# Retention projections of two heads as seven block products over half of the depth

## The reference, cut to what matters

```python
h = rms_norm(x, norm1_g)
proj = h @ w_in                     # 2048 x 7168: retention q,k,v,gate and attention q,k,v, 8 heads of 128 each
rq, rk, rv, rg, aq, ak, av = split(proj)
ret = silu(rg) * head_group_norm(retention(rotary(rq), rotary(rk), rv), ret_norm_g)
att = chunk_attention(rms_norm(aq, q_norm_g), rms_norm(ak, k_norm_g), av, rel_bias)
x = x + concat([ret, att]) @ w_out
h = rms_norm(x, norm2_g)
x = x + square(relu(h @ w_ff1)) @ w_ff2      # 2048 -> 8192 -> 2048
```

## Time and profile before

| what | value |
|---|---|
| time, median of 3 runs | 1113.13 us (1112.95 to 1113.15) |
| the profiled execution's own time | 1113.28 us |
| its span, first to last instruction | 1111.2 us |
| around the span | 2.1 us |
| busy share of PE, DVE, ACT, POOL | 99%, 75%, 59%, 5% |
| granted TensorE clock, mean | 1.000 |
| moved by DMA | 253 MB, 228 GB/s over the span |

### The profile page before, as it was taken

The page is one execution under the profiler, slowest core; times in us unless marked ns, Lnnn a source line. Parts: engine busy times, 40 slices in busy tenths (PEclk is TensorE's granted clock), DMA queues, the critical chain, the costliest instruction groups (busy, mean ns, idle before and its releaser), DMA issues.

```text
span 1111.2 us, 13678 instructions
## 1 busy us (share of the span) xinstructions
PE 1105.2 (99%) x5234; PEld 942.2 (85%) x5234; DVE 830.8 (75%) x828; ACT 657.3 (59%) x765; POOL 51.5 (5%) x58
## 2 busy tenths in 40 slices
PE   9999999999999999999999999999999999999998
PEld 8889899899898888888888888888888888888887
DVE  6667566576576668869787869787869787869783
ACT  6544544554554556677655577665577665577662
POOL 0100000000000000000000000000000000000000
PEclk9999999999999999999999999999999999999999
DMA  9855455454464556787797787797787797787792
GB/s 362 319 191 180 151 198 179 151 197 153 156 217 152 204 208 182 266 278 220 246 290 222 258 277 221 243 291 221 259 279 220 244 291 221 259 277 219 246 278 86
DMA packets 39551, 253.14 MB, mean 228 GB/s; under 512 B 4432, under 2 KB 4944, under 8 KB 12624
## 3 DMA queue, kind: packets, MB, share of 16 engines
q1 hardware_dynamic: 34464, 218.12, 53.4%
q0 software_dynamic: 4608, 33.56, 16.0%
q10 hardware_dynamic: 432, 0.81, 0.2%
HBM read 250.37 MB, written 2.10 MB: 227 GB/s over the span
## 4 chain that ended last, share of the span: by engine, by line
PE 99%; DMA 0%; ACT 0%; DVE 0%; ACTq 0%; issue 0%
PE acc L489 11%; PE acc L496 11%; PE acc L503 11%; PE acc L667 10%; PE acc L665 10%; PE acc L663 10%; PE bankC L643 4%; PE acc L643 4%; PE acc L638 4%; PE bankC L638 4%; PE bankC L636 4%; PE acc L636 4%; PE bankD L643 1%; PE bankD L638 1%; PE bankD L636 1%; PE acc L687 1%
## 5 line engine op out<-in xcount | busy, mean ns | idle before, releaser
L1311 DVE TENSOR_TENSOR w_lo<-raw,w_hi 128x2048 fp32r<-128x2048 f32 x180 | 410.9, 2289 | 126.8 <-ACT w_hi L924 126.6
L924 ACT ACTIVATE w_hi<-raw 128x2048 fp32r<-128x2048 f32 x180 | 344.8, 1917 | 220.8 <-PE acc L667 145.9
L1118 DVE TENSOR_TENSOR w_lo<-raw,w_hi 128x1024 fp32r<-128x1024 f32 (+1 forms) x152 | 167.8, 1107 | 68.6 <-ACT w_hi L767 68.5
L767 ACT ACTIVATE w_hi<-raw 128x1024 fp32r<-128x1024 f32 (+1 forms) x152 | 142.9, 962 | 34.3 <-PE acc L503 25.3
L489 PE MATMUL acc<-w_hi,hT_hi 128*128 128x512 f32 (+1 forms) x512 | 129.5, 374 | 0.8 <-ACT w_hi L767 0.8
L496 PE MATMUL acc<-w_hi,hT_lo 128*128 128x512 f32 (+1 forms) x512 | 123.5, 362 | 0.0
L503 PE MATMUL acc<-w_lo,hT_hi 128*128 128x512 f32 (+1 forms) x512 | 123.2, 362 | 0.0
L496 PEld LDWEIGHTS acc<-w_hi,hT_lo 128*128 128x128 f32 x512 | 93.5, 188 | 10.5
L503 PEld LDWEIGHTS acc<-w_lo,hT_hi 128*128 128x128 f32 x512 | 93.4, 188 | 10.0
L663 PE MATMUL acc<-w_hi,hF_hi 128*128 128x512 f32 x256 | 100.8, 394 | 0.0
L663 PE MATMUL acc<-w_hi,dF_hi 128*128 128x512 f32 x256 | 99.9, 390 | 0.0
(11 more groups left out here) (187 smaller groups left out, 1573.4 us busy)
## 6 DMA issues: line engine op xcount, KB each, us to landing
raw<-in_w_up SPq DMA_DIRECT2D x64, 1024.0 KB, 6.4
raw<-in_w_down SPq DMA_DIRECT2D x64, 1024.0 KB, 6.5
raw<-in_w_ret SPq DMA_DIRECT2D x32, 1024.0 KB, 4.7
raw<-in_w_att SPq DMA_DIRECT2D x28, 768.0 KB, 4.4
raw<-in_w_out SPq DMA_DIRECT2D x16, 1024.0 KB, 4.7
raw<-in_w_up POOLq DMA_DIRECT2D x16, 1024.0 KB, 8.6
raw<-in_w_down POOLq DMA_DIRECT2D x16, 1024.0 KB, 8.9
raw<-in_w_att SPq DMA_DIRECT2D x6, 384.0 KB, 7.7
```

Of the source, the lines that this page charges most:

```text
L767: nc.scalar.activation(piece(w_hi, q, 0, PIECE_KT * n), raw[:, q // 2, (q % 2) * PIECE_KT * n:(q % 2 + 1) * PIECE_KT * n], ACT.Copy).then_ ...
L924: nc.scalar.activation(w_hi[:, ring(s)], raw[:, r, :], ACT.Copy).then_inc(slab_hi, 1)
L1118: nc.vector.tensor_tensor(piece(w_lo, q, 0, PIECE_KT * n), raw[:, q // 2, (q % 2) * PIECE_KT * n:(q % 2 + 1) * PIECE_KT * n], piece(w_hi, ...
L1311: nc.vector.tensor_tensor(w_lo[:, ring(s)], raw[:, r, :], w_hi[:, ring(s)].bitcast(f32), ALU.subtract).then_inc(slab_lo, 1)
```

## The change

Attention projections stay as they are. The retention projections of two heads (blocks of the loop `i` in 0 to 3) are now computed together. The part of them over depth tiles 0 to 7 is a 2 by 2 block of weight slabs, a and b above, e and d below (a and e belong to the first column block, b and d to the second), and takes seven products of 12 matmuls: Q1 (a), P5 (a+b), P6 (a+b+d), P7 (b+d), P3 (d), Q2 (e), P4 (a+b+d+e). Each writes a single bank. Depth tiles 8 to 15 are computed as before, with 24 matmuls a slab: Z1, Z2 for one head, H1, H2 for the other. A block runs these 19 slabs, 38 pieces, on every engine:

```diff
+        def in_free(i, step, m):
+            ...
+            elif step == "P5":
+                pe.wait_ge(sf_lo_ok, 1)
+                if i:
+                    pe.wait_ge(p5_kept, i)
+            elif step == "P6":
+                pe.wait_ge(sf_lo_ok, 2)
+                pe.wait_ge(q1_kept, i + 1)
+            elif step == "P7":
+                pe.wait_ge(sf_lo_ok, 3)
+                pe.wait_ge(z_set, i + 1)
+            elif step == "P3":
+                pe.wait_ge(sf_lo_ok, 4)
+            elif step == "Z1" and m == 1:
+                pe.wait_ge(w_set, i + 1)
+            elif step == "Q2":
+                pe.wait_ge(h_set, i + 1)
+            elif step == "P4":
+                pe.wait_ge(y_set, i + 1)
...
+                for bank, m in banks:
+                    if half == 0:
+                        in_free(i, step, m)
+                    for t in tiles:
+                        fresh = step in ("I0", "J0", "Q1", "P5") and t == 0
+                        wide = N if fresh else n
+                        start = (t - 2 * half) * n
+                        nc.tensor.matmul(bank[:, 0:wide], stationary(step, m, t)[0], piece(w_hi, q, start, start + wide),
+                                         start=fresh, stop=False, skip_group_check=True)
...
+            def in_hi(q):
+                i, step, half = in_step(q)
+                ...
+                elif half == 0 and step == "P5":
+                    act.wait_ge(in_summed, 4 * i + 1)
+                elif half == 0 and step == "P6":
+                    act.wait_ge(in_summed, 4 * i + 2)
+                elif half == 0 and step == "P7":
+                    act.wait_ge(in_summed, 4 * i + 3)
+                elif half == 0 and step == "P4":
+                    act.wait_ge(in_summed, 4 * i + 4)
...
+            def in_sum(i, into, other, read):
+                r, o = IN_PLAN[i, into][0], IN_PLAN[i, other]
+                dve.wait_ge(in_raw[o[0]], o[1])
+                dve.wait_ge(lo_done, in_first(i, read) + 2)
+                nc.vector.tensor_tensor(raw[:, r, :], raw[:, r, :], raw[:, o[0], :], ALU.add).then_inc(in_summed, 1)
...
+                at_piece(i, 10, att_mean_squares, h)
+                at_piece(i, 10, in_sum, i, "a", "b", "Q1")
...
+            load_group(G_OUT, w_out, 0, N)
+            sp.wait_ge(piece_used, in_first(BLOCKS - 1, "P3") + 2)
+            for c in range(OUT_GROUPS):
+                sp.dma_start(xs[:, :, c * N:(c + 1) * N], x_rows[:, :, c * N:(c + 1) * N]).then_inc(x_in[c], 16)
...
+            def last_slab(p, step):
+                ...
+                for m, bank, first, end in ((0, bH, 0, N), (1, bY, 0, half), (1, bX, half, N)):
+                    for t in range(SLAB_KT):
+                        cols = slice(t * N + first, t * N + end)
...
+                    dve.wait_ge(half_used, 2 * prev + 4)
+                    both = xs[:, 1, c * N:(c + 1) * N]
+                    nc.vector.tensor_tensor(both, bY[:], both, ALU.add).then_inc(acc_read_dve, 1)
+                    dve.wait_ge(acc_read_dve, added(prev) + 4)
+                    dve.wait_ge(slab_used, slab_no(prev, "H2") + 1)
+                    right = xs[:, 1, c * N + half:(c + 1) * N]
+                    nc.vector.tensor_tensor(right, bX[:, half:N], right, ALU.add).then_inc(acc_read_dve, 1)
```

More of the change, by code:

```diff
@@ L419, in _ @@
             for p in (PAIRS - 2, PAIRS - 1):
-                for n in range(4):
+                for n in range(4 if p < PAIRS - 1 else 3):
                     c, m = 2 * (p % 2) + (n < 2), n % 2
@@ L423, in _ @@
                     sp.dma_start(out_rows[:, m, c * N:(c + 1) * N], xs[:, m, c * N:(c + 1) * N]).then_inc(stored, 16)
-            sp.wait_ge(stored, 4 * MT * 16)
+            for half in range(2):
+                first = (OUT_GROUPS - 2) * N + half * (N // 2)
+                sp.wait_ge(acc_read_dve, added(PAIRS - 1) + 4 + half)
+                sp.dma_start(out_rows[:, 1, first:first + N // 2], xs[:, 1, first:first + N // 2]).then_inc(stored, 16)
+            sp.wait_ge(stored, (4 * MT + 1) * 16)
         @block.gpsimd
@@ new lines, in _ @@
+            for q in range(8 * G_OUT):
+                nxt = q + AHEAD
+                if nxt < PIECES:
+                    x_hi(nxt)
+                if nxt < 8 * G_OUT:
+                    in_hi(nxt)
+                else:
+                    hi_piece(G_OUT, nxt - 8 * G_OUT, N)
+                if q == PIECES:
+                    act.wait_ge(gq_ok, 1)
+                for f in work.get(q, ()):
+                    f()
+            group(G_OUT, N, N, {j: work.get(8 * G_OUT + j, []) for j in range(PIECES)})
```

622 lines of the change are left out of this document (440 added, 182 removed).

## The result

The changed kernel takes 1137.84 us (median of 4 runs, 1137.68 to 1138.35), the kernel before 1113.07 (1112.95 to 1113.15): a ratio of 1.0223, 95% interval 1.0206 to 1.0241. It is 24.8 us slower. The forecast was 1134.8, in a range of 1119 to 1145.

The account below looks back on a forecast made before the run. TensorE, busy 1105.2 of 1111.2 us, was taken as the bound. From 1113.3: -10.0 for matmuls, +23.2 for block waits, +8.7 for the first block, -0.4 at the end gave 1134.8 us, range 1119 to 1145.

Parts of the forecast that it names:

- C: Transposes of each block's first retention head: TensorE waits for VectorE's rotation and addition, 1.9 us a block.
- A: Transposes of each block's first attention head: TensorE waits for scaled q and k behind sum a+b, 1.3 us.
- low part 25: Around Z1: TensorE waits for VectorE's low part of piece 25, made after the fourth sum, 0.6 us a block.
- bank subtraction: Z1's second row tile: TensorE waits for VectorE's subtraction after the low part of piece 26, 0.9 us a block.
- The block without waits: Block of two heads with fewer matmuls and no new waits: 82.7 us against 85.2, kernel 10.0 us less.
- The first block: Activation sums at pieces 8 to 15 add waits of 3.5 and 4.5 us and small ones: +8.7 us.
- The tail: Program's end: narrower last matmuls +0.2 us, shorter last add and store, net -0.4 us (-0.7 to +1.2).
- The signs: In the profile: some 32 us of TensorE waits on VectorE, blocks about 88.5 us, VectorE near 85%, feed-forward unchanged.
- Waits hidden: Rival: VectorE and ScalarE running ahead of TensorE cover the blocks' waits, time 1102.9 us; chance 0.10.
- B: Around Z1: TensorE waits 0.6 us for low part 25, 0.9 for the bank subtraction, 0.7 for scaled q and k.
- Slabs late: Rival: slab e lands late in each block, lengthening the wait around Z1, +7 us, 1142; chance 0.12.
- The clock falls: Rival: in the first block TensorE's long standstills bring 1.2 GHz for pieces 12 and 13, up to +8 us; chance 0.10.

Follow-up runs that it names:

- the kernel with every order mended: Changed kernel with rotation, fourth sum, activation sums, both heads' squares and scaling, and softmaxes all moved, nothing left out: 1115.88 us, ratio 1.0025.
- the kernel with the new first block: The kernel with every order mended, plus ScalarE, GpSimd and VectorE steps of its first block reordered: 1112.60 us, ratio 0.9996.

## Why the prediction was right, step by step

**Direction and mechanism: right.** The matmuls removed were worth less than the waits that the added work made, with VectorE busy 80% on average. Runs showed it, not the trace alone: with the same matmuls and the waits mended the time falls by 26.9 us (1137.84 to 1110.90), which is more than the 24.8 lost. Of the orders turned alone, C gave 7.4 us and the activation sums 5.1, both about as expected.

**The waits of a block: right in sum, and nearly one by one.** Measured as the distance beyond the usual spacing in the second block: A 1.35 (forecast 1.3), first softmax 0.27 (0.3), low part 25 0.66 (0.6), bank subtraction 0.73 (0.9), second head's q and k 0.57 (0.7), second softmax 0.23 (0.1), C 1.96 (1.9). The sum is 5.77 against 5.8. That it agrees to 0.03 is luck, since single steps are off by up to 0.2.

**The block without waits: this term was too small.** I put it at 82.7 us, from matmul counts times spacing. The block is 89.3 with 5.8 of waits, so 83.5 without. The kernel whose one labelled wait is 0.22 us still takes 83.96, or 83.7 without it. So the removed matmuls were worth 1.5 to 1.7 us a block and not 2.5, which is some 3.2 us over four blocks and about as much as the forecast was short (1137.8 - 1134.8 = 3.0). Part of it can be seen: a product's piece of six matmuls takes 1.37 to 1.39 us and not 1.36, and behind each wait the first matmuls of a piece are up to 0.1 us further apart. The rest lies in steps of 0.1 that I did not assign, so it stays open.

**The first block: right within 1 us, in part by luck.** From the same point of the program it takes 98.7 us, against a forecast of 97.2; 0.8 of the difference is the block's base. Its two long waits come where they were walked: 3.2 us (forecast 3.5), and 3.5 for a_qk (4.5). At full clock the second would have been 5.3, since the slow piece 12 fills 1.8 us of it; the scaling came late because VectorE waited 0.91 us for GpSimd's power, which the walk has as covered. The slow clock adds 1.4 us behind it, which the sum has at nothing, and so the smaller waits must be below the 2.3 us put for them. These errors nearly cancel.

```profile
35.23 0.73 PE L740 MATMUL bankC<-w_lo,hT_hi 128*128 128x512 f32 x2 [3.17 <-DVE w_lo L1393]
35.99 1.51 PE L727 MATMUL acc<-w_hi,hT_hi 128*128 128x384 f32 x4
...
43.43 0.69 PE L612 MATMUL bankA<-ident,a_qk 128*128 128x128 f32 x2 [3.52 <-DVE a_qk L1476]
```

**The tail: right.** The matmuls of 256 columns stand 0.120 us apart in the kernel after, and its end is 0.3 us shorter than before (forecast 0.4). The edit alone in the kernel before gives 0.65 us, inside the bounds of the term, but there the store gave 0.6, more than the 0.4 allowed for it.

**The signs.** From its first product to the end of the span the feed-forward stage takes 688.9 us (689.2 before), as forecast. VectorE is busy 81% between 100 and 350 us, not near 85%. The profile's list has 24.0 us of waits and not 32, since it counts idle time alone: in the second block it has 1.16 for A and 1.79 for C, where the distances have 1.35 and 1.96.

**The rivals.** *Waits hidden*: no, and the one thing it claimed, that a lead covers them, failed at A, B and C alike. *Slabs late*: no, VectorE waited 0.3 us once for the DMA of a retention slab in the whole run. *The clock falls*: it did, with 0.66 and 0.70 granted behind the two long waits, so part of TensorE's time there is at 1.2 GHz. I gave it 0.10, and it came; its price was what I had wrong. I put up to 8 us on it. Piece 12 took 3.9 us and not 2.1, but behind it TensorE waited for a_qk in any case. Only piece 13 and the transposes counted, 1.4 us, and of these 0.7 came back when the clock was held up. The Trainium skill (TensorE: Matmul & The Clock Gate, "Why this matters for your kernels") had warned of this. The trace agrees that the clock falls behind idle gaps. The rule says nothing of where the slow matmuls lie.

**What I read as price and was not.** The prediction treats A, B and C as separate waits with separate causes. C was one. A and B were not: mending the order at A, squares and power included, gave 1.0 us of 6, and at B 1.4. Only the kernel with every order mended got A's stretch down to one wait of 0.65 us and B's to none. The size of a wait told what it cost, not what its removal gives.

## What to carry to other kernels

A mean load of 80% told nothing here, since the work comes in bursts. Walk one period in each engine's queue order, with the producing chain over all engines, and sum the waits; here that gave 5.8 us a block and the trace 5.77. When such waits are to be removed, look at the whole period at once: four single edits gave 14.9 us in sum, and the kernel with them and the rest of the period mended gave 22.0. Taking work off one engine helps only if the chain doesn't run over the engine that gets it: fill the gaps of the chain first.

## What the hardware showed beyond that

**GpSimd's power depends on what VectorE does beside it.** The same instruction (128x4) took 1.01 us with VectorE idle in the kernel with the scaling first, 2.98 in the changed kernel, where it begins beside a sum, and 4.46 in its first block, where a sum, a low part and an activation sum's low part follow each other. In the kernel before it was 1.91, begun beside a low part.

```profile
129.61 1.01 POOL L532 TENSOR_TENSOR a_rs<-a_ms,neg_half 128x4 f32<-128x4 f32 x1 [8.61 <-DVE a_ms L1469]
```

```profile
38.01 4.46 POOL L532 TENSOR_TENSOR a_rs<-a_ms,neg_half 128x4 f32<-128x4 f32 x1 [2.75 <-DVE a_ms L1469]
...
130.10 2.98 POOL L532 TENSOR_TENSOR a_rs<-a_ms,neg_half 128x4 f32<-128x4 f32 x1 [8.61 <-DVE a_ms L1469]
```

In the first block this counted: VectorE waited 0.91 us for it ahead of the scaling. So a small GpSimd step costs more here just where VectorE works on two tiles from SBUF, and adding such work to VectorE lengthens the chain twice. The Trainium skill (SBUF — State Buffer, "SBUF: two separate sides") says that a VectorE instruction with two SBUF inputs and a GpSimd one that reads SBUF take turns at one pair of ports, each for its whole duration. The trace agrees in direction: the power ends 0.86 us after the low part beside which it began in the kernel before (118.45 and 119.31 us), 0.86 after the sum in the changed kernel (132.22 and 133.08), and 0.89 after the last of the three in its first block (41.58 and 42.47). But no VectorE instruction is seen to wait for GpSimd: a low part of 128x768 that starts beside the power in the kernel with the new first block takes 0.96 us, as elsewhere. Records on GpSimd are rough, so whether they take turns stays open.

**The clock fell behind two waits of 3.2 and 3.5 us** (0.66 and 0.70 granted in the windows after them) and not behind those of 2 us or less in the later blocks. Work of no use in the same waits kept it at 1.00. A single long wait was not needed for it: in the kernel with the first head's squares earlier, two waits of 1.2 and 1.9 us with four matmuls between them were followed by 0.50 from 35 to 40 us, and in the kernel with all orders mended 1.2 and 2.5 us by 0.66. In the one with the new first block, whose longest wait is 1.2 us, it stayed at 1.00.
